# Products that nobody reads at the norms between the stages of a two-block transformer kernel

## The chip, the core and the metric

The kernel runs on one core of a Trainium2 chip. Five engines work side by side, each in its own program order, and wait for one another by semaphores: TensorE (PE, with its weight loads shown as PEld), VectorE (DVE), ScalarE (ACT), GpSimd (POOL) and SyncE (SP), which issues transfers. Matrix products land in PSUM, eight banks of 128 x 512 f32. TensorE's clock is granted at one of two levels, 2.4 and 1.2 GHz; the profile gives it as a share, 1.00 or 0.50. The metric is the time of one execution on the device in microseconds (us), lower is better.

## The reference

Two layers of a hybrid block (sliding-window attention beside an RWKV-7 mix, a gated FFN with a short convolution, and a gated embedding), then two layers of a second block (a pooling mixer beside latent attention, and a squared-ReLU FFN), then a last norm. There are 512 tokens of 1024 channels, all in f32. The norms and where they stand:

```python
def rmsnorm(x, g):
    y = xf * lax.rsqrt(jnp.mean(xf * xf, axis=-1, keepdims=True) + NORM_EPS)
    return y * g
# first block, per layer
h = rmsnorm(x, norm_mix_pre);  ... mixed from h ...
x = x + rmsnorm(mixed @ w_out, norm_mix_post)
h = rmsnorm(x, norm_ffn_pre);  ... u, ua, ub from h @ w_up ...
x = x + rmsnorm((gelu(ua) * ub) @ w_down, norm_ffn_post)
x = x + rmsnorm(sigmoid(x @ w_ple_gate) * (p_i @ w_ple), norm_ple)
# second block, per layer
h = rms_norm(x, ln1_g) * (1 + sc1) + sh1;  ...
x = x + g1 * (merged @ w_out)
h2 = rms_norm(x, ln2_g) * (1 + sc2) + sh2
x = x + g2 * (square(relu(h2 @ w_ff1)) @ w_ff2)
# at the end
rms_norm(x, final_g)
```

## The kernel before

Activations lie transposed: 8 tiles of 128 channels x 512 tokens (`xT`, `hh`, `hl`). Each f32 product is made of three: an operand is split into a high part (`hh`, `Whi`, rounded) and a low part (`hl`, `Wlo`, the rest), and TensorE adds high x high, low x high and high x low (L231). One weight tile of 128 x 1024, called a unit here, gives one output tile: 8 channel tiles by 3 products of 128 x 512, 24 in all. Units come from HBM in a fixed order (`raw`, issued by SP, L308); ACT makes `Whi` (L283) and GpSimd `Wlo` (L298), three slots deep. A first GEMM behind a norm takes two units at once (`split_pair`): per channel tile 6 products as soon as the `hl` of this tile is there, 48 in all; the 49th is the first of the third unit.

A norm goes through four engines:

- ACT squares a tile (L132, L161); TensorE sums it over channels by 16 one-column instructions per tile (`column_sums`, L177, into bank 7). Where a GEMM's outputs are summed (n2, n4, n5, and nx of the second block), DVE adds up six of the tiles first and TensorE has three groups of 16. At n3 and at nx of the first block there is one group per tile, eight in all, each behind the residual's tile (DVE L1812 and L1815).
- ACT takes the root (L145), DVE the reciprocal (L216, for nx L223).
- TensorE spreads the 4 columns of 1/root over a bank by four transposes (`norm_spread_pe`, L204, bank 6).
- DVE scales a tile (L391), ACT rounds it to `hh` (L364 or L366), DVE makes `hl` (L382 or L385): the split.

The names are n1 (before the mix), n2 (behind it in the first block, before the FFN in the second), n3 (before the FFN, first block), n4 (behind the FFN), n5 (behind the embedding's gate) and nx, the sums of the next layer's n1. Between nx and n1 a program block ends: all engines meet at a barrier, semaphores are cleared, and only then come n1's spread and the first weight loads of the new block. Behind n4 the products of `ph` and `pl` with the embedding's weights follow, which don't need the norm.

The order on each engine is the order in which the code is written; TensorE executes in that order, waits included.

Of the kernel before, what the change touches and what calls it, by code (L numbers as in the profile page):

```python
# [26 lines left out]
P = 128  # L27
# [3 lines left out]
KD = D // P  # L31
# [9 lines left out]
ADA_W, ADA_K = 512, 2  # L41
ADA_N = KD // ADA_K
MOD_BANK = 6


HEADS, KV, HD = 16, 4, 64
# [132 lines left out]
    return last  # L179


def norm_sum_pe(pe, s, b, name, i, n):

    pe.wait_ge(s[name + "_sq"], i + 1)
    column_sums(pe, b, b["sq"][:, i % 2], i == 0, i == n - 1).then_inc(s[name + "_ss"], 1)


def summed_squares_pe(pe, s, b, name):

    pe.wait_ge(s[name + "_ac"], KD - 3)  # L190
    column_sums(pe, b, b["sacc"], True, False)
    for i in (KD - 2, KD - 1):
        pe.wait_ge(s[name + "_sq"], i + 1)
        last = column_sums(pe, b, b["sq"][:, i % 2], False, i == KD - 1)
    last.then_inc(s[name + "_ss"], 1)


def norm_spread_pe(pe, s, b, name):

    if name != "n1":  # L200
        pe.wait_ge(s[name + "_rs"], 1)
    rt = b["rtn" if name == "n1" else "rt"]
    for c in range(BLK):
        last = pe.transpose(b["rstd"][:, c * P:(c + 1) * P], rt[:, c:c + 1].broadcast_to([P, P]), b["c"]("ident"))  # L204
    last.then_inc(s[name + "_sp"], 1)


def norm_pe(pe, s, b, name, n):
    for i in range(n):
        norm_sum_pe(pe, s, b, name, i, n)  # L210
    norm_spread_pe(pe, s, b, name)


def norm_dve(dve, s, name, b):
# [21 lines left out]
def tiles_of(high, low):  # L236

    return (lambda k: high[:, k]), (lambda k: low[:, k])
# [1817 lines left out]
def first_block(nc, b, stream, stream_after, ple, ada, positions):  # L2056
# [6 lines left out]
    with ExitStack() as ctx:  # L2063
        s, every = semaphores(ctx, nc, names)
# [42 lines left out]
        for layer in range(LAYERS):  # L2107
            enter_layer(b, layer, stream[layer], stream[layer + 1] if layer + 1 < LAYERS else stream_after[0])
            with nc.Block() as block:
# [50 lines left out]
                @block.tensor  # L2160
                def _(pe):
                    ring = Ring(s, b)
                    h = tiles_of(b["hh"], b["hl"])
                    norm_spread_pe(pe, s, b, "n1")
                    rwkv_pe(pe, s, b, ring)
                    pe.wait_ge(s["post_a"], POST_A(PAIRS - 1, "sd"))
                    attention_pe(pe, s, b, ring)
                    gated_pe(pe, s, b, ring, ((h, None), (h, None), (tiles_of(b["aoh"], b["aol"]), (s["ao_lo"], PAIRS)),
                                              (tiles_of(b["yrh"], b["yrl"]), (s["y_back"], 32 * PAIRS))))
                    pe.wait_ge(s["gate_a"], 16)  # L2170
                    project_pe(pe, s, b, ring, s["wo_p"], s["wo_z"], s["mx_lo"], "n2")
                    norm_spread_pe(pe, s, b, "n2")
                    norm_pe(pe, s, b, "n3", KD)
                    ffn_pe(pe, s, b, ring)
                    norm_spread_pe(pe, s, b, "n4")
                    for m in range(KD):
                        if m % 4 == 0:
                            w = ring.take(pe)
                        if m == 0:
                            pe.wait_ge(s["p_lo"], 1)  # L2180
                        if m >= 4:
                            pe.wait_ge(s["e_z"], m - 3)
                        split_matmuls(pe, b["ps"][:, m % 4], columns_of(w, 2, width=512, j=m % 4 * P), tiles_of(b["ph"], b["pl"]), 2) \
                            .then_inc(s["e_p"], 1)
                    pe.wait_ge(s["e_z"], 6)
                    project_pe(pe, s, b, ring, s["pg_p"], s["pg_z"], s["h3_lo"], "n5", (s["e_z"], KD))
                    norm_spread_pe(pe, s, b, "n5")
                    for i in range(KD):
                        norm_sum_pe(pe, s, b, "nx", i, KD)

                @block.scalar
                def _(act):
# [123 lines left out]
def second_pe(pe, s, b):  # L2316
    ring = Ring(s, b)
    norm_spread_pe(pe, s, b, "n1")
    pair = [ring.take(pe) for _ in range(2)]
    split_pair(pe, s["h1_lo"], [b["ps"][:, i] for i in range(2)], pair, b, s["z_p"])  # L2320

# [85 lines left out]
    gated2_pe(pe, s, b, ring)  # L2407
    pe.wait_ge(s["gate_a"], 16)
    project_pe(pe, s, b, ring, s["wo_p"], s["res1"], s["mx_lo"], "n2")
    norm_spread_pe(pe, s, b, "n2")  # L2410
    for key in FFN2[0]:
        if key[0] == "up":
            i = key[1]
            if i == 0:
                pair = [ring.take(pe) for _ in range(2)]
                split_pair(pe, s["h2_lo"], [b["ps"][:, x] for x in range(2)], pair, b, s["f1_p"])
            if i < 2:
                continue
            w = ring.take(pe)
            if i >= 4:  # L2420
                pe.wait_ge(s["f1_a"], i - 3)
            split_product(pe, b["ps"][:, i % 4], w, b).then_inc(s["f1_p"], 1)
        elif key[1] == PARTS2 - 1 and key[2] < OPEN:
            if key[2] == 0:
                last_down_pe(pe, s, b, ring, FT2)
        else:
            down_pe(pe, s, b, ring, key[1], key[2], FT2)
            if key[1] == PARTS2 - 1 and key[2] == KD - 1:
                summed_squares_pe(pe, s, b, "nx")


def gated2_pe(pe, s, b, ring):
# [690 lines left out]
```

## Time and profile before

| | us |
|---|---|
| median of 3 runs | 3971.61 |
| lowest and highest | 3971.05, 3975.33 |
| the profiled execution | 3976.66 |
| its span, first to last instruction | 3974.8 |
| TensorE busy (matmul) | 3763.6 |
| VectorE, ScalarE, GpSimd busy | 1909.9, 1601.3, 1716.6 |
| mean granted clock of TensorE | 0.973 |

A time line has a row for each run of like instructions: start, length, engine, source line, operation, output and inputs, sizes and count; in brackets the idle time before it and what ended that. A run of products is pipelined: the last one's tail is part of the row's length. A table of stretches gives the busy time of each engine in a stretch with the number of instructions, and the granted clock.

### The profile page before, as it was taken

What the parts mean: (1) busy time and instruction counts of PE and PEld (TensorE: products, weight loads), DVE (VectorE), ACT (ScalarE), POOL (GpSimd) and SP (SyncE); (2) the same over time, 40 slices, a digit from 0 to 9 for tenths busy, and PEclk for the clock granted to TensorE, in tenths of its full rate; (3) what the DMA queues carried; (4) which work ended last, traced back from release to release, by engine and by line L of the source; (5) the groups of instructions that cost most, each with busy time, mean ns of one, the idle gap of its engine ahead of it and who ended that gap; (6) DMA issues with size and microseconds to landing.
All of it is one profiled execution on the core that took longest, in us unless ns stands there. A gap on an engine that the chain in (4) does not pass through costs nothing. (4 is left out here: it accounts for less than half of the span.)

```text
span 3974.8 us, 71522 instructions
## 1 busy us (share of the span) xinstructions
PE 3763.6 (95%) x30328; PEld 3070.8 (77%) x30328; DVE 1909.9 (48%) x2978; ACT 1601.3 (40%) x2675; POOL 1716.6 (43%) x1088
## 2 busy tenths in 40 slices
PE   7999979999998999997999999899999999999998
PEld 6777758878887777776887888677878877787887
DVE  7777682255535767768215563535231123423112
ACT  5555353343334555526234233444332234433222
POOL 4555413434445555531443444453444435344443
PEclk9999989989999999998998999899999999999999
DMA  4111203235532211121433553221323322232332
GB/s 136 52 54 55 87 27 133 94 127 186 189 106 85 91 50 56 55 86 26 137 100 135 184 190 101 80 74 60 94 91 96 100 85 69 64 96 89 97 96 85
DMA packets 108749, 379.81 MB, mean 96 GB/s; under 512 B 12560, under 2 KB 12944, under 8 KB 107792
## 3 DMA queue, kind: packets, MB, share of 16 engines
q1 hardware_dynamic: 102816, 365.66, 28.5%
q10 hardware_dynamic: 5616, 9.58, 0.7%
q8 instruction: 241, 3.95, 0.4%
q14 instruction: 76, 0.62, 0.0%
HBM read 359.46 MB, written 15.73 MB: 94 GB/s over the span
## 5 line engine op out<-in xcount | busy, mean ns | idle before, releaser
L298 POOL TENSOR_TENSOR Wlo<-raw,Whi 128x1024 fp32r<-128x1024 f32 (+1 forms) x744 | 1383.0, 1871 | 1945.5 <-ACT Whi L283 1945.3
L231 PE MATMUL ps<-hh,Whi 128*128 128x512 f32 x2864 | 1152.2, 402 | 32.0 <-DVE hl L382 10.1
L231 PE MATMUL ps<-hl,Whi 128*128 128x512 f32 x2864 | 1126.1, 393 | 0.0
L231 PE MATMUL ps<-hh,Wlo 128*128 128x512 f32 x2864 | 1125.5, 393 | 0.1
L283 ACT ACTIVATE Whi<-raw 128x1024 fp32r<-128x1024 f32 x552 | 580.8, 1056 | 691.6 <-PE ps L231 618.0
L231 PEld LDWEIGHTS ps<-hh,Whi 128*128 128x128 f32 x2864 | 543.5, 190 | 161.5 <-issue 29.8
L231 PEld LDWEIGHTS ps<-hh,Wlo 128*128 128x128 f32 x2864 | 543.4, 190 | 115.9 <-issue 0.5
L231 PEld LDWEIGHTS ps<-hl,Whi 128*128 128x128 f32 x2864 | 544.2, 190 | 107.9 <-issue 1.9
L231 PE MATMUL ps<-gh,Whi 128*128 128x512 f32 x864 | 338.1, 391 | 4.1 <-POOL Wlo L298 4.1
L231 PE MATMUL ps<-gh,Wlo 128*128 128x512 f32 x864 | 336.6, 390 | 0.0
L231 PE MATMUL ps<-gl,Whi 128*128 128x512 f32 x864 | 336.6, 390 | 0.0
L1757 DVE TENSOR_TENSOR sg<-sg,ps 128x512 f32<-128x512 f32 x64 | 44.1, 688 | 369.5 <-PE ps L231 369.2
L1136 POOL TENSOR_TENSOR TM<-TD,const 128x256 f32<-128x256 f32 x192 | 162.8, 871 | 78.0 <-PE ps L718 43.8
L231 PEld LDWEIGHTS ps<-gh,Whi 128*128 128x128 f32 x864 | 162.3, 188 | 39.4 <-POOL Wlo L298 6.2
L231 PEld LDWEIGHTS ps<-gh,Wlo 128*128 128x128 f32 x864 | 162.3, 188 | 33.7
L231 PEld LDWEIGHTS ps<-gl,Whi 128*128 128x128 f32 x864 | 162.3, 188 | 33.2
L2688 DVE SCALAR_TENSOR_TENSOR xT<-ps,mod,xT 128x512 f32<-128x512 f32 x64 | 48.1, 752 | 281.1 <-PE ps L231 281.1
L1950 ACT ACTIVATE acc<-ps,par 128x512 f32<-128x512 f32 x88 | 68.6, 780 | 273.7 <-PE ps L231 273.7
L2678 DVE TENSOR_TENSOR gt<-gt 128x512 f32<-128x512 f32 x64 | 47.9, 749 | 256.9 <-ACT gt L2566 256.9
L2001 DVE SCALAR_TENSOR_TENSOR acc<-ps,par,acc 128x511 f32<-128x511 f32 x88 | 66.0, 750 | 198.0 <-ACT acc L1950 198.0
L1740 ACT ACTIVATE sg<-ps 128x512 f32<-128x512 f32 x64 | 38.3, 599 | 239.2 <-PE ps L231 239.2
L2566 ACT ACTIVATE gt<-ps 128x512 f32<-128x512 f32 x64 | 38.3, 598 | 213.0 <-PE ps L231 213.0
(360 smaller groups left out, 5746.3 us busy)
## 6 DMA issues: line engine op xcount, KB each, us to landing
raw<-in_stream SPq DMA_DIRECT2D x554, 512.0 KB, 3.6
ada<-in_ada SPq DMA_DIRECT2D x96, 512.0 KB, 4.5
park_x<-xT SPq DMA_DIRECT2D x2, 2048.0 KB, 7.2
park_yh<-yh ACTq DMA_DIRECT2D x16, 256.0 KB, 2.1
park_yl<-yl ACTq DMA_DIRECT2D x16, 256.0 KB, 2.4
xT<-park_x SPq DMA_DIRECT2D x2, 2048.0 KB, 8.2
yrh<-park_yh SPq DMA_DIRECT2D x16, 256.0 KB, 5.1
yrl<-park_yl SPq DMA_DIRECT2D x16, 256.0 KB, 5.2
```

The source lines that it names most:

```text
L231: last = pe.matmul(ps, left[a](k), right[c](k), start=start and k == 0 and i == 0, stop=stop and k == n - 1 and i == 2)
L283: act.activation(self.b["Whi"][:, weight_slot(self.b, u)], self.b["raw"][:, raw_slot(self.b, u)], ACT.Copy).then_inc(self.s["w_hi"], 1)
L298: last = pool.tensor_tensor(b["Wlo"][:, slot, part], b["raw"][:, raw_slot(b, u), part], b["Whi"][:, slot, part].bitcast(F32), SUB)
L1136: pool.tensor_tensor(blocks(b["TM"][:, h, l % 2]), blocks(b["TD"][:, h]), lvl[:, l].broadcast_to([P, BLK, CB]), MUL) .then_inc(s["inv_g"], 1)
L1740: act.activation(b["sg"][:, i], b["ps"][:, i], ACT.Sigmoid).then_inc(s["gate_a"], 1)
L1757: dve.tensor_tensor(b["sg"][:, i], b["sg"][:, i], b["ps"][:, 4 + i], MUL).then_inc(s["gate_v"], 1)
L1950: act.activation(b["acc"][:, slot], b["ps"][:, slot], ACT.Identity, scale=b["p"]("cw2", j * FT + i), bias=b["p"]("cb", j * FT + i)).then_i ...
L2001: dve.scalar_tensor_tensor(out=b["acc"][:, slot, 1:TOK], in0=b["ps"][:, slot, 0:TOK - 1], scalar=b["p"]("cw1", j * FT + i), in1=b["acc"][: ...
L2566: act.activation(b["gt"][:, i % 4], b["ps"][:, i % 4], ACT.Relu).then_inc(s["f1_a"], 1)
L2678: dve.tensor_tensor(b["gt"][:, i % 4], b["gt"][:, i % 4], b["gt"][:, i % 4], MUL).then_inc(s["f1_v"], 1)
L2688: dve.scalar_tensor_tensor(out=b["xT"][:, m], in0=b["ps"][:, 4 + i % 3], scalar=b["mod"][:, 40 + m:41 + m], in1=b["xT"][:, m], op0=MUL, op ...
```

## The change

A helper `idle_products` issues n products of two constants (the identity and a tile of ones, 128 x 128 each, f32) into PSUM bank 5, columns 0 to 127. Nothing reads them, and they wait for nothing. They stand at three kinds of place: 6 between the last column sum of a norm and what waits for its root (`IDLE_ROOT`), 4 before each column sum of n3 and of the first block's nx, 10 before the first of them (`IDLE_SUM`, and two thirds of `IDLE_SPLIT`), and 16 between a spread and the first GEMM product behind it (`IDLE_SPLIT`). That is 154 per layer of the first block and 44 per layer of the second, 396 in all. No other instruction changes, on any engine.

```diff
+IDLE_BANK = 5
+IDLE_ROOT, IDLE_SUM, IDLE_SPLIT = 6, 4, 16
+def idle_products(pe, b, n):
+    for _ in range(n):
+        pe.matmul(b["ps"][:, IDLE_BANK, 0:P], b["c"]("ident"), b["c"]("ones"), start=True, stop=True)
-def norm_pe(pe, s, b, name, n):
+def idle_sums_pe(pe, s, b, name, n):
     for i in range(n):
+        idle_products(pe, b, 2 * IDLE_SPLIT // 3 if i == 0 else IDLE_SUM)
         norm_sum_pe(pe, s, b, name, i, n)
-    norm_spread_pe(pe, s, b, name)
+    idle_products(pe, b, IDLE_ROOT)
...
                     norm_spread_pe(pe, s, b, "n1")
+                    idle_products(pe, b, IDLE_SPLIT)
                     rwkv_pe(pe, s, b, ring)
...
                     project_pe(pe, s, b, ring, s["wo_p"], s["wo_z"], s["mx_lo"], "n2")
+                    idle_products(pe, b, IDLE_ROOT)
                     norm_spread_pe(pe, s, b, "n2")
-                    norm_pe(pe, s, b, "n3", KD)
+                    idle_sums_pe(pe, s, b, "n3", KD)
+                    norm_spread_pe(pe, s, b, "n3")
+                    idle_products(pe, b, IDLE_SPLIT)
                     ffn_pe(pe, s, b, ring)
+                    idle_products(pe, b, IDLE_ROOT)
                     norm_spread_pe(pe, s, b, "n4")
+                    idle_products(pe, b, IDLE_SPLIT)
...
                     project_pe(pe, s, b, ring, s["pg_p"], s["pg_z"], s["h3_lo"], "n5", (s["e_z"], KD))
+                    idle_products(pe, b, IDLE_ROOT)
                     norm_spread_pe(pe, s, b, "n5")
-                    for i in range(KD):
-                        norm_sum_pe(pe, s, b, "nx", i, KD)
+                    idle_sums_pe(pe, s, b, "nx", KD)
...
# second block
     norm_spread_pe(pe, s, b, "n1")
+    idle_products(pe, b, IDLE_SPLIT)
...
     project_pe(pe, s, b, ring, s["wo_p"], s["res1"], s["mx_lo"], "n2")
+    idle_products(pe, b, IDLE_ROOT)
     norm_spread_pe(pe, s, b, "n2")
+    idle_products(pe, b, IDLE_SPLIT)
...
                 summed_squares_pe(pe, s, b, "nx")
+                idle_products(pe, b, IDLE_ROOT)
```

TensorE before, in the first block from the end of the mix's projection over n2 and n3 to the first GEMM of the FFN (`sacc` and `sq` are the squares, `rt` the reciprocal root, `hh`, `hl`, `Whi`, `Wlo` the parts):

```order
L177 MATMUL ps<-const,sacc 64x1 x8
L177 MATMUL ps<-const,sq 64x1 x16
L204 MATMUL ps<-const,rt 128x128 x4
L177 MATMUL ps<-const,sq 64x1 x64
L204 MATMUL ps<-const,rt 128x128 x4
L231 MATMUL ps<-hh,Whi 128x512
```

The same place now; L187 are the new products, and L177, L204 and L231 are L179, L212 and L240:

```order
L179 MATMUL ps<-const,sacc 64x1 x8
L179 MATMUL ps<-const,sq 64x1 x16
L187 MATMUL ps<-const 128x128 x6
L212 MATMUL ps<-const,rt 128x128 x4
L187 MATMUL ps<-const 128x128 x10
L179 MATMUL ps<-const,sq 64x1 x8
L187 MATMUL ps<-const 128x128 x4
...
L187 MATMUL ps<-const 128x128 x6
L212 MATMUL ps<-const,rt 128x128 x4
L187 MATMUL ps<-const 128x128 x16
L240 MATMUL ps<-hh,Whi 128x512
```

Nothing changed its order; every spread, every column sum from n3's first on and the first GEMM product stand behind a set of new products. At a block's end, here between nx of the second layer and n1 of the second block (the two branches are the end of one program block and the start of the next, with the barrier between them), the six stand before the barrier:

```order
L179 MATMUL ps<-const,sq 64x1 x8
L187 MATMUL ps<-const 128x128 x6
L2118 UNCONDITIONAL_BRANCH
L2823 UNCONDITIONAL_BRANCH
L212 MATMUL ps<-const,rtn 128x128 x4
L187 MATMUL ps<-const 128x128 x16
L240 MATMUL ps<-hh,Whi 128x512
```

Before, the column sums were TensorE's last work ahead of that barrier.

## Rows read from the trace of the kernel before

**Rows 1.** The page: the span, and TensorE's clock in 40 slices.
```profile
span 3974.8 us, 71522 instructions
...
PEclk9999989989999999998998999899999999999999
```

**Rows 2.** Time line, TensorE: spreads of n2, n4 and n5, five of eight.
```profile
821.68 1.12 PE L204 MATMUL ps<-const,rt 128*128 128x128 f32 x4 [0.58 <-DVE rt L216]
...
1281.62 0.65 PE L204 MATMUL ps<-const,rt 128*128 128x128 f32 x4 [0.57 <-DVE rt L216]
...
2103.35 0.65 PE L204 MATMUL ps<-const,rt 128*128 128x128 f32 x4 [0.58 <-DVE rt L216]
...
2498.06 1.12 PE L204 MATMUL ps<-const,rt 128*128 128x128 f32 x4 [0.58 <-DVE rt L216]
...
2910.90 1.12 PE L204 MATMUL ps<-const,rt 128*128 128x128 f32 x4 [0.65 <-DVE rt L216]
```

**Rows 3.** Stretches of time: busy time of each engine, and the clock.
```profile
core 0: us, PE busy (x) PEld busy (x) DVE busy (x) ACT busy (x) POOL busy (x), PEclk, DMA share, GB/s
2907.20:2910.50 3.30, 2.58 (x53) 1.97 (x51) 0.82 (x2) 0.83 (x2) 0.00 (x0) 1.00 0.55 159
2910.60:2920.70 10.10, 7.26 (x19) 5.54 (x20) 8.45 (x13) 4.27 (x6) 0.00 (x0) 0.50 0.01 2
821.60:845.40 23.80, 15.97 (x149) 13.38 (x150) 18.75 (x30) 9.08 (x15) 0.00 (x0) 0.50 0.06 21
```

**Rows 4.** Time line at n2 of the second block, layer 1.
```profile
2909.62 0.63 PE L177 MATMUL ps<-const,sq 128*64 128x1 f32 x16 [0.48 <-ACT sq L161]
...
2914.56 0.77 PE L231 MATMUL ps<-hh,Whi 128*128 128x512 f32 x1 [2.54 <-DVE hl L382]
...
2924.21 2.40 POOL L298 TENSOR_TENSOR Wlo<-raw,Whi 128x1024 fp32r<-128x1024 f32 x1 [17.89 <-ACT Whi L283]
...
2928.45 0.39 PE L231 MATMUL ps<-hh,Whi 128*128 128x512 f32 x1
```

**Rows 5.** Time line, TensorE, at n3 of the first block, layer 1.
```profile
825.03 1.02 PE L177 MATMUL ps<-const,sq 128*64 128x1 f32 x16 [2.23 <-ACT sq L132]
...
831.94 1.02 PE L177 MATMUL ps<-const,sq 128*64 128x1 f32 x16 [0.36 <-ACT sq L132]
...
839.81 0.77 PE L231 MATMUL ps<-hh,Whi 128*128 128x512 f32 x1 [2.39 <-DVE hl L385]
...
853.46 0.39 PE L231 MATMUL ps<-hh,Whi 128*128 128x512 f32 x1
```

**Rows 6.** Attention: f32 products on the time line, and stretches as in rows 3.
```profile
2685.27 4.03 PE L2403 MATMUL ps<-PT,vtok 128*64 128x128 f32 x20
...
2685.30:2688.60 3.30, 3.30 (x17) 3.30 (x17) 3.23 (x9) 1.97 (x7) 3.06 (x4) 0.50 0.00 0
2688.70:2692.00 3.30, 3.29 (x17) 2.03 (x15) 3.30 (x7) 1.09 (x5) 3.05 (x4) 1.00 0.00 0
558.80:562.00 3.20, 3.20 (x20) 2.87 (x22) 3.17 (x4) 1.60 (x3) 0.00 (x0) 0.50 0.00 0
562.20:565.50 3.30, 2.65 (x34) 1.98 (x30) 3.20 (x7) 3.02 (x13) 0.00 (x0) 1.00 0.00 0
```

**Rows 7.** Time line between nx of layer 1 and n1 of layer 2.
```profile
1295.54 0.18 DVE L223 RECIPROCAL rtn<-rtn 128x4 f32<-128x4 f32 x1 [2.08 <-ACT rtn L145]
...
1297.13 1.09 PE L204 MATMUL ps<-const,rtn 128*128 128x128 f32 x4 [1.93 <-PEq L117]
...
1305.32 0.69 DVE L385 TENSOR_TENSOR hl<-t,hh 128x512 fp32r<-128x512 f32 x1
...
1307.32 2.40 DVE L385 TENSOR_TENSOR hl<-t,hh 128x512 fp32r<-128x512 f32 x1 [0.53 <-ACT hh L366]
```

**Rows 8.** Time line behind n4's spread, layer 1.
```profile
1217.30 2.35 POOL L2151 TENSOR_TENSOR pl<-pT,ph 128x1024 fp32r<-128x1024 f32 x1 [4.29 <-ACT ph L2222]
1217.55 2.65 DVE L1815 TENSOR_TENSOR xT<-xT,t 128x512 f32<-128x512 f32 x1
```

## Prediction, before the changed kernel was run

> **What bounds the kernel now.** I read the page first [rows 1]: the span is 3974.8 us, and TensorE's granted clock is below full speed in some slices only. The profiled execution took 3976.66 us, 5.05 us above the median of the three timed runs (3971.61); every difference below is worked out inside the profiled execution and then laid on that median. Second, the time line of the eight spreads of n2, n4 and n5, of which five stand in [rows 2]: four transposes took 0.65 us where the clock was 2.4 GHz, and 1.11 or 1.12 us where it was 1.2 (at half clock also those at 2562.94 and 3604.20, at full that at 1216.08). Third, busy time and clock by stretch [rows 3]: from 821.6 to 845.4 and from 2910.6 to 2920.7 the clock stood at 0.50, although VectorE, not TensorE, sets the pace of most of it. What that costs is the part where TensorE has the 48 products of the first two weight tiles to do. In the first block they began at 839.81 and the 49th began at 853.46 [rows 5], 13.65 us, of which 5.6 us (839.81 to 845.4) at 1.2 GHz. If a product takes p at full and 2p at half clock, 5.6/2p + 8.05/p = 48, so p = 0.226 us, and 48 at full clock would be 10.85 us. Behind that pair TensorE is back to back, so what is gained or lost at the 49th product is carried on.
>
> **What one of the new products costs.** Nobody waits for them, but TensorE works in order, so whatever stands behind them waits. None of that shape (128x128 by 128x128, f32) is in the trace. Nearest is the run of 20 f32 instructions with 128 columns at 2685.27 [rows 6], 4.03 us, of which 3.38 us at half clock: 16 at 0.214 is 3.4, four at 0.109 is 0.4, plus a tail of 0.2. An f32 product in the source is two such instructions, so a product is 0.22 us at full clock and 0.43 at half. The transposes bound it from the other side: 0.65 against 1.12 us for four [rows 2] gives 0.118 each. A set of 6 is thus 1.3 (2.6) us, of 16 3.5 (6.9), of 10 2.2 (4.3), of 4 0.87 (1.7). Column sums of one tile: 0.63 us at full and 1.02 at half [rows 4, 5], 0.48 and 0.9 without the tail.
>
> **Can they hold the clock?** In the stretch before 2910.5 TensorE counted as busy 2.58 of 3.30 us at clock 1.00 [rows 3], and yet it fell: what ran last were 48 one-column sums, and the longest idle piece shown there is 0.48 us [rows 4]. The Trainium skill says in "TensorE: Matmul & The Clock Gate", section "Why this matters for your kernels", that throughput is kept by leaving no long idle gap between bursts; by that rule the norms would be cured by any instruction stream and the sum would be the "held" one below, 3966. The trace does not agree that gaps decide. I take from the rows that column sums do too little, and that products of this kind do enough, since the clock rose from 0.50 to 1.00 while the 20 instructions of [rows 6] ran. But the six products come only behind the last sum. In five of the eight spreads the transposes already ran at half clock [rows 2]: there the fall came within 0.6 us of the last sum (2910.90 less 0.65 is the sum's end, the fall was at 2910.5), before the six can have done much. In the other three it came behind the spread, and there they can prevent it. So each place has two ends, held and fallen.
>
> **Second block, n2 (twice).** Held: the six start at 2910.1 and end at 2911.4; the spread waits for them instead of the reciprocal, and takes 0.65 instead of 1.12, so it ends at 2912.05 against 2912.02. The sixteen fill 2911.8 to 2915.3; the first GEMM product starts 0.7 us later than 2914.56 [rows 4]. 48 at 0.226 end at 2926.1, but the low part of the third tile is there only at 2924.21 + 2.40 = 2926.6 [rows 4]: 2926.7 against 2928.45, a gain of 1.75; layer 2 alike, 1.6. Fallen: two of the six at full clock, four at 0.43, a spread of 1.12: it ends at 2913.35, 1.35 late; VectorE's chain and the third tile move with it, 2928.0 against 2928.45, a gain of 0.45, and in layer 2 a loss of 0.2.
>
> **First block, n2 and n3 (twice).** The residual hands a tile to the sums every 1.38 us (1.02 busy and 0.36 idle [rows 5]); sums and four products at full clock are 0.48 + 0.87 = 1.35, so they just fit. The ten before the first sum fit its wait of 2.2 us (825.03). The last sums are 0.4 us shorter, the six delay the spread by 0.6 and it is 0.45 shorter: end 0.2 earlier. The sixteen let the first product start at 840.5, 48 end at 851.4 against 853.46: gain 2.0. In layer 2 the clock had risen sooner by itself: gain 1.0. Fallen at n2: the spread is 1.3 to 1.8 us late, the sixteen run at full clock again: gain 0.5 and 0.
>
> **Block ends (three into an n1, one into the last norm).** The barrier waits for the last engine. That was VectorE's reciprocal at 1295.54, and the spread came at 1297.13 [rows 7]. Now TensorE's six end later than that, by 0.6 to 1.0 us. Behind the barrier the weight loads start too, and one split step waits for them and then beside GpSimd (2.40 us at 1307.32, where the one before took 0.69 [rows 7]), so a faster TensorE gains little there. Held: losses 0.2, 0, 0.1 and 0.4, in all 0.7. Fallen: the six take 2.6, and at n5 the spread and the residuals behind it are late too: 2.7, 2.2, 1.9 and 1.9, in all 8.7.
>
> **Before the e products (n4, twice).** The spread comes 0.55 us later at full clock. It costs nothing: VectorE's second step there was stuck beside GpSimd's subtraction anyway (2.65 us at 1217.55, against 2.35 us from 1217.30 [rows 8]). Fallen, the spread is 1.8 us late and the first product 2.9: 1.3 each, 2.6. **Start:** sixteen products at half clock delay the first GEMM by 2 to 4 us, but they also bring the rise forward: loss 0.2, between 0 and 1.0.
>
> **Sum.** All held: -6.4 + 0.7 + 0 + 0.2 = -5.5, or 3966.1. All fallen: -(0.5 + 0 + 0.45 - 0.2) + 8.7 + 2.6 + 1.0 = +11.5, or 3983.1. Falling where it fell before: first block -1.3 (between its ends, since 821.68 ran at half clock but the fall came late) and -1.0, second block -0.45 and +0.2, block ends +0.2, +2.2, +0.3, +0.4, n4 0 and +1.3, start +0.2: +2.05. The place of the fall is not tied to the program: the same norm of the two layers ran its spread at 1.12 (821.68) and at 0.65 us (2103.35) [rows 2]. So I lean a little to the middle of the ends (+3.0): +2.4, 3974.0 us. On the profiled execution's own time that is 3979.1.
>
> **Rivals.** (1) *Held everywhere*, 3966.1. For it: three of the eight spreads at full clock. Against: in five the fall comes with the last sum. (2) *Fallen everywhere*, 3983.1. (3) *Slower: the clock stays down through the sums of n3 or nx.* Sums and four products at half clock are 0.9 + 1.7 = 2.6 us against the 1.38 that VectorE gives; seven times 1.25 is 8.7 us, and with the late spread 12 us at each of four norms: 3986 for one, 4022 for all. It decides at one point: whether the clock is up again before the first sum. Against it: six products, spread and ten products are 7.7 us without a gap at half clock, more than the 5.6 us that GEMM products needed. The Trainium skill says in the same page, Part 4, that transposes do not count as activity for the clock; by that rule the spread breaks this run and the rival is likelier. The trace speaks against it: from 558.8 to 562.0 only transposes and short f32 products ran, at clock 0.50, and from 562.2 on it was 1.00 [rows 6]. (4) *The products don't count for the clock at all:* then all sums run so, some 4050; the 20 instructions of [rows 6] speak against it.
>
> **Chances.** Mixed falls, as forecast: 0.55 (3970 to 3979). Held: 0.17. Fallen everywhere or nearly: 0.18. Low clock through sums: 0.08. Not counted: 0.02. A measurement here can tell about 0.2%, 7.9 us. Held comes to -5.5, inside it; I give faster 0.12 for errors in my terms. Slower is the upper half of fallen, rivals 3 and 4 and a little of the mixed case: 0.26. Same: 0.62. The range reaches from held to fallen: 3966 to 3984.
>
> **What the changed kernel's profile would show.** Product groups of 16 lasting 3.5 us (6.9 if at half clock); spreads of 0.65 us; sums and four products every 1.38 us with TensorE idle under 0.1; clock 1.00 from n3's first sum to the split and 10.9 us for 48 products, with a wait for the third tile's low part in the second block. At block ends TensorE, not VectorE, is last at the barrier, and the spread follows the reciprocal by 2.2 us or more instead of 1.6. Wrong I would be if the clock fell inside the sums, or if it held at all of the five early places, or if a product took much more than 0.22 us.

## The result, and the profile after

The changed kernel takes 3994.02 us (median; 3988.5 to 3997.57) beside 3973.47 for the kernel before: 1.0054 times as long, 95% interval 1.0042 to 1.0066. It is 21 us slower, outside the predicted range (3966 to 3984). The profiled execution took 3992.09 us, its span is 3989.6.

The page of the changed kernel, span and granted clock in 40 slices, answers to [rows 1]:
```profile
span 3989.6 us, 73106 instructions
...
PEclk9999989999999999998999999999999999999999
```
Of five slices that stood at 8 three are at 9; the mean clock rose from 0.973 to 0.987. So the change did what it says, and the kernel got slower all the same. The clock was not the thing to look at; the time between two marks in the program was.

TensorE at n2 and n3 of the first block, layer 1 (start us, us, then as in [rows 2]; L187 are the new products, two instructions each, L179 the column sums, L212 a spread, L240 GEMM products):
```profile
825.14 2.29 PE L187 MATMUL ps<-const 128*128 128x128 f32 x12
827.22 1.06 PE L212 MATMUL ps<-const,rt 128*128 128x128 f32 x4
828.08 2.98 PE L187 MATMUL ps<-const 128*128 128x128 f32 x20
...
832.64 0.63 PE L179 MATMUL ps<-const,sq 128*64 128x1 f32 x16
833.20 1.16 PE L187 MATMUL ps<-const 128*128 128x128 f32 x8
834.29 0.63 PE L179 MATMUL ps<-const,sq 128*64 128x1 f32 x16
...
842.54 0.63 PE L179 MATMUL ps<-const,sq 128*64 128x1 f32 x16
843.11 1.60 PE L187 MATMUL ps<-const 128*128 128x128 f32 x12
...
844.55 0.60 PE L212 MATMUL ps<-const,rt 128*128 128x128 f32 x4
...
848.48 0.47 PE L240 MATMUL ps<-hh,Whi 128*128 128x512 f32 x1
...
859.48 0.39 PE L240 MATMUL ps<-hh,Whi 128*128 128x512 f32 x1
```
Read the starts, 832.64 and 834.29: a tile of sums and its four products take 1.65 us, where VectorE hands over a tile every 1.38 [rows 5]. The last line is the 49th product: 11.00 us after the first, 13.65 before [rows 5]. So 2.65 us are won there, and by then 4.56 have been lost. Layer 1, each step counted from the one before it and set against the same step of before, by the starts: n2's spread +1.43 from its first sum (the six, half of them at 1.2 GHz); the first sum of n3 0.42 further (the ten); seven intervals of 1.65 instead of 1.38, +1.87; n3's spread +0.42 (the six); the first GEMM product +0.43 (the sixteen); the 49th -2.65. In all +1.92.

The stretches, as in [rows 3]:
```profile
826.00:842.50 16.50, 16.50 (x199) 15.47 (x198) 10.88 (x16) 5.04 (x8) 0.00 (x0) 0.90 0.08 26
842.50:859.40 16.90, 16.90 (x113) 14.97 (x113) 11.06 (x17) 6.67 (x11) 2.39 (x1) 1.00 0.00 1
```
TensorE had no idle time left in the sums, at a clock of 0.90. In [rows 3] it was busy for 15.97 of 23.8 us, at 0.50. From the engine that waited it has become the bound.

The first block end (n5, nx, n1 of layer 2), layer 1:
```profile
1287.37 1.02 PE L179 MATMUL ps<-const,sq 128*64 128x1 f32 x16 [1.69 <-ACT sq L163]
1288.31 2.93 PE L187 MATMUL ps<-const 128*128 128x128 f32 x12
1291.03 1.06 PE L212 MATMUL ps<-const,rt 128*128 128x128 f32 x4
...
1307.10 1.61 PE L187 MATMUL ps<-const 128*128 128x128 f32 x12
...
1310.09 0.62 PE L212 MATMUL ps<-const,rtn 128*128 128x128 f32 x4 [1.38 <-PEq L119]
...
1320.73 0.39 PE L240 MATMUL ps<-hh,Wlo 128*128 128x512 f32 x1
1323.82 0.50 PE L240 MATMUL ps<-hh,Whi 128*128 128x512 f32 x1 [2.71 <-DVE hl L394]
```
The clock had fallen at n5's last sum: the six took 2.93 us and the spread, itself at half clock, comes 2.46 later than 1281.62 [rows 2]. nx's spread is 3.56 later still. Behind it TensorE, at full clock, has done 30 of the pair's 48 products by 1321, those of five channel tiles, and waits 2.7 us for the sixth tile's low part. VectorE could start on that only behind ACT's rounding (2.13 us idle), which in turn stood behind the split of a weight tile that had waited for its transfer, and then took 2.35 us for it beside GpSimd, as in [rows 7]:
```profile
1319.74 1.06 ACT L292 ACTIVATE Whi<-raw 128x1024 fp32r<-128x1024 f32 x1 [2.55 <-DMA raw<-in_stream]
...
1321.42 2.35 DVE L394 TENSOR_TENSOR hl<-t,hh 128x512 fp32r<-128x512 f32 x1 [2.13 <-ACT hh L375]
```
Right behind this wait the clock fell once more; the stretches with the clock:
```profile
1320.80:1324.20 3.40, 0.69 (x4) 0.34 (x3) 2.74 (x2) 1.04 (x3) 2.34 (x1) 1.00 0.00 0
1324.30:1327.50 3.20, 3.20 (x9) 2.43 (x8) 1.54 (x3) 0.63 (x1) 0.10 (x1) 0.50 0.42 159
```
The 49th product is 1.88 us later relative to the first, not 2.65 earlier. This block end costs 8.5 us: 2.46 and 3.56 for the two spreads, 0.56 for the sixteen behind the second, and 1.88.

### The profile page after: what moved, and what is told of

It reads as the page before. It is cut to its first block and busy times, and to the rows that moved or that the text cites. A ratio compares the mean times of both kernels' runs of the same rounds, so it can differ in the third digit from the quotient of the medians.

```text
span 3989.6 us, 73106 instructions
## 1 busy us (share of the span) xinstructions
PE 3828.5 (96%) x31120; PEld 3141.4 (79%) x31120; DVE 1902.8 (48%) x2978; ACT 1601.8 (40%) x2675; POOL 1715.7 (43%) x1088
## 5 line engine op out<-in xcount | busy, mean ns | idle before, releaser
L240 PE MATMUL ps<-hh,Whi 128*128 128x512 f32 x2864 | 1144.3, 400 | 16.9 <-ACT wS L893 9.3
L240 PE MATMUL ps<-hl,Whi 128*128 128x512 f32 x2864 | 1118.8, 391 | 0.0
L240 PE MATMUL ps<-hh,Wlo 128*128 128x512 f32 x2864 | 1118.7, 391 | 0.0
L240 PEld LDWEIGHTS ps<-hh,Whi 128*128 128x128 f32 x2864 | 538.9, 188 | 143.0 <-issue 18.9
L240 PEld LDWEIGHTS ps<-hh,Wlo 128*128 128x128 f32 x2864 | 539.0, 188 | 114.3 <-issue 0.2
L240 PEld LDWEIGHTS ps<-hl,Whi 128*128 128x128 f32 x2864 | 539.5, 188 | 106.8 <-issue 1.9
L240 PE MATMUL ps<-gh,Whi 128*128 128x512 f32 x864 | 337.9, 391 | 3.8 <-POOL Wlo L307 3.8
L240 PE MATMUL ps<-gh,Wlo 128*128 128x512 f32 x864 | 336.5, 390 | 0.0
L240 PE MATMUL ps<-gl,Whi 128*128 128x512 f32 x864 | 336.5, 389 | 0.0
L240 PEld LDWEIGHTS ps<-gh,Whi 128*128 128x128 f32 x864 | 162.2, 188 | 38.9 <-POOL Wlo L307 5.5
L240 PEld LDWEIGHTS ps<-gh,Wlo 128*128 128x128 f32 x864 | 162.2, 188 | 33.7
L240 PEld LDWEIGHTS ps<-gl,Whi 128*128 128x128 f32 x864 | 162.2, 188 | 33.4
L727 PEld LDWEIGHTS ps<-X,TM 64*64 64x64 f32 x2560 | 82.0, 135 | 54.1 <-issue 29.6
```

Source lines behind the costliest of these rows:

```text
L240: last = pe.matmul(ps, left[a](k), right[c](k), start=start and k == 0 and i == 0, stop=stop and k == n - 1 and i == 2)
L727: return pe.matmul(b["ps"][half(u), bank, block(c)], left[:, block(c)], right[:, block(c)], start=True, stop=True)
```

## The experiments

Every kernel here is told by five numbers: how many products stand behind the very first spread (start), between the last sum and a spread (six), ahead of the first sum of n3 and nx (ten), ahead of each other sum (four), and between a spread and the first GEMM product (sixteen). The first and the last are one constant (`IDLE_SPLIT`) in all kernels but g1, g2 and g3. The edit is small, for instance of the run with three in place of four:
```
-IDLE_ROOT, IDLE_SUM, IDLE_SPLIT = 6, 4, 16
+IDLE_ROOT, IDLE_FIRST, IDLE_SUM, IDLE_SPLIT = 6, 10, 3, 16
...
-        idle_products(pe, b, 2 * IDLE_SPLIT // 3 if i == 0 else IDLE_SUM)
+        idle_products(pe, b, IDLE_FIRST if i == 0 else IDLE_SUM)
```
In g1, g2 and g3 a constant of its own stands behind n1's spread in the first block, and that line is run for both layers: g1 and g3 have the sixteen at the start and behind n1 of layer 2 (g1's trace has 64 instructions of these products, the last at 1302.6 us), g2 lacks them at both. Where their expectations say "the very first spread", read both.

"Norms" below is worked out from a kernel's trace: the times of the marks (first sum or first spread of a norm to the 49th product behind it, with the start and the end of the program) against those of the first trace of before, summed over all norms. "Rest" is the same for all else, where the change puts nothing. The ratio is to before on the same chip.

| kernel | start, six, ten, four, sixteen | median us | ratio (95%) | norms | rest |
|---|---|---|---|---|---|
| before, second trace | 0 0 0 0 0 | 3967.3 (one) | | +0.5 | -9.8 |
| changed | 16 6 10 4 16 | 3994.0 | 1.0054 (1.0042 to 1.0066) | +17.9 | -3.1 |
| e6, changed again | the same | 4000.4 (one) | | +23.0 | +0.8 |
| g4, a third time | the same | 3997.9 | 1.0065 (1.0051 to 1.0078) | +21.6 | +1.5 |
| e1 | 16 6 10 0 16 | 3994.7 | 1.0056 (1.0038 to 1.0074) | +19.5 | -1.2 |
| e2 | 16 6 10 2 16 | 4008.3 | 1.0082 (1.0067 to 1.0098) | +25.4 | +6.9 |
| e7 | 16 6 10 3 16 | 3980.2 | 1.0023 (1.0013 to 1.0033) | +9.1 | -7.2 |
| f2 | 16 6 10 8 16 | 4020.8 (one) | | +47.1 | -3.0 |
| f3 | 0 0 0 4 0 | 4011.7 (one) | | +43.3 | -8.3 |
| f1 | 0 6 0 0 0 | 3987.1 | 1.0035 (1.0023 to 1.0047) | +15.8 | -4.7 |
| e3 | 16 0 10 4 16 | 3986.0 | 1.0033 (1.0023 to 1.0044) | +9.9 | -1.2 |
| e4 | 16 0 0 0 16 | 3979.1 | 1.0013 (1.0003 to 1.0022) | -0.4 | -7.5 |
| e8 | 8 0 0 0 8 | 3965.4 | 0.9987 (0.9977 to 0.9996) | -7.9 | -8.7 |
| f4 | 8 0 10 3 8 | 3970.1 | 0.9991 (0.9982 to 1.0000) | -3.7 | -3.0 |
| g1 | 16 (and at n1 of layer 2) 0 0 0 0 | 3976.4 | 1.0007 (0.9998 to 1.0016) | +0.2 | -5.9 |
| g2 | 0 (nor at n1 of layer 2) 6 10 4 16 | 3992.5 | 1.0048 (1.0032 to 1.0063) | +12.2 | +6.5 |
| g3, g1 again | the same as g1 | 3973.4 (one) | | +1.0 | -4.2 |

**What repeats and what does not.** Two traces more of the two kernels, unchanged.

> The kernel before, unchanged, for a second trace. The question is what the stretches that the change does not touch do between two executions of one program. In the traces so far the start of the first column sum at the end of the attention (819.05 us in before) moved by +0.5 to +7.0 us between kernels, measured from the 49th product of the first stage, and that of the second layer (2100.72) by -0.8 to -6.8. Theory A (where the clock falls in those stretches is chance): the two marks move by up to 6 us here too, and the norms by less than 0.5 us each. Theory B (the change moves them): both marks stay within 1 us of before's first trace.

> The changed kernel, unchanged, for a second trace. Theory A (losses at the norms are the pace of TensorE and repeat, the rest is chance): the spread of n3 and nx comes again 2.7 to 3.6 us late against before, the gain at the following 48 products is again 2.1 to 2.6 us wherever the third tile is there, all norms together +15 to +19 us, and the attention stretches differ from the first trace by up to 6 us. The loss of 1.88 us behind the first block end's n1 (1300 to 1314 us) is a second fall of the clock while TensorE waited; it may or may not repeat. Theory B (the places of the falls make the loss): the norms' sum differs by more than 5 us between the two traces.

In before's second trace the norms sum to within 0.5 us of the first, though two of them moved more than theory A allowed (-0.9 and +1.1 in the second block); elsewhere it differs by 9.8, 5.8 of it in the second attention alone, while the first ended 0.6 late. Of the 5.8, 3.6 lie at one place: in the first trace TensorE stood still for 1.83 us there, for nothing that the profile shows, and the clock fell right behind it; in the second trace neither happened. The row and the stretch in before, then the same stretch in its second trace:
```profile
1417.81 0.33 PE L718 MATMUL ps<-XT,Wc 64*64 64x64 f32 x4 [1.83 <-issue]
...
1418.90:1422.30 3.40, 3.40 (x9) 2.63 (x8) 3.36 (x6) 0.95 (x3) 1.61 (x3) 0.50 0.22 41
```
```profile
1418.90:1422.30 3.40, 3.40 (x123) 2.75 (x125) 3.37 (x6) 3.12 (x7) 3.40 (x4) 1.00 0.00 0
```
The changed kernel's n2 and n3 of layer 1 cost +1.9 in all three traces, of layer 2 +2.9, the first block end +8.5, +8.4, +8.8. Between the three, norms differ by up to 5.1 us, at block end 2 and the last norm above all, where the six ran at full or at half clock. That is just past the 5 us of theory B, and +23.0 and +21.6 lie above the 19 and 20 us that theory A gave. So the larger part of the norms' loss, about 18 us, is of the kernel and repeats (theory A), up to 5 us hang on where the clock falls, and a single trace's rest is of the execution. The column "norms" also follows the measured medians: sums of 3, 4 and 8, +9.1, +20.8 (the mean of three) and +47.1, against +9, +21 to +26 and +49 us beside before. It does not replace them: e2's and g2's medians lie 8 us above their norms, and the traced executions of e4 and e8 were the fastest of ten, 10 and 5 us below the median.

**Between the sums.** Four runs vary this number, one has it alone.

> The changed kernel without the four products between the column sums of n3 and nx (seven times four at each of four norms); the ten before the first sum, the six and the sixteen stay. In the changed kernel's trace each sum with its four products takes 1.65 us, where the residual gives a tile every 1.385: 7 to 8 times 0.27, 2.1 us per norm, 8.5 in all. Theory A (the sums' pace is the largest mis-sized term): 8 us below the changed kernel, about 3986; or a little less gain if the clock falls during the sums, since a sum at half clock (1.02) still fits 1.385. Theory B (what costs is the six products that stand before spreads and barriers): no change, 3994.

> The changed kernel with two products instead of four between the sums. At full clock a sum is 0.48, two products 0.44 and the switch between them 0.28: 1.2, which fits 1.385; at half clock 0.9 + 0.85 + 0.3 = 2.0, which does not. Theory A: 8 us below the changed kernel, 3986, with the spread behind the sums at full clock (0.65). Theory B: 3994. If the clock falls in the sums it is above 3994.

> As the changed kernel, with three products in place of four between the column sums of n3 and nx. In the changed kernel a tile of sums took 1.65 us (0.63 to 0.65 the sums, 0.89 four products, the rest in going from one to the other), where VectorE hands one over every 1.38 us. Theory A (the pace of TensorE there is the loss): with three, 1.65 - 0.22 = 1.43 us a tile, 0.05 above VectorE's, so seven intervals cost 0.3 in place of 1.9 us at each of the four norms; the spread of n3 comes 1.0 us late in place of 2.7, and if the clock holds the kernel takes 6 to 7 us less than the changed one, 3987. Theory B (three leave the clock to fall, as two did, and then sums and products run at half clock, 2.6 us or more a tile with three): as slow as with two, 4000 to 4008, spread of n3 3 to 4 us late.

> The changed kernel with eight products in place of four between column sums. The suspected cost doubled: four took 1.65 us a tile, three 1.43, so a product is 0.22 and the sums with the turn from one kind to the other are 0.76. Theory A: eight give 0.76 + 1.78 = 2.54 us a tile, at each of the four norms seven intervals of 2.54 - 1.65 = 0.89, 6.2 us more than the changed kernel, 25 us in all, so 4012 to 4028 (executions of one kernel differ by up to 8 us); the clock holds through the sums. Theory B (not the pace of TensorE but the places of the clock's falls make the loss): no more than 10 us above the changed kernel.

> The kernel before with four products ahead of each column sum of n3 and nx but the first, and none elsewhere. Theory A (the pace is the loss, whatever surrounds it): if the clock is up or comes up during the first tiles, 1.65 us a tile, the spreads of n3 and nx 1.9 to 2.6 us late; if it is down at the first sum it takes 2.6 us a tile or more until it rises, up to 4 us late. The first GEMM product behind them then starts at full clock and gives 2.6 us back per place where VectorE lets it: between -1 and +2 us at each of the four places, 0 to +6 in all. Theory B (the clock does not rise at all on four products and sums): 2.6 us a tile throughout, 8 us and more at each of the four, over 30 us in all.

TensorE in n3 of layer 1, with three products (e7), with eight (f2):
```profile
829.58 0.63 PE L179 MATMUL ps<-const,sq 128*64 128x1 f32 x16
830.14 0.94 PE L187 MATMUL ps<-const 128*128 128x128 f32 x6
831.00 0.63 PE L179 MATMUL ps<-const,sq 128*64 128x1 f32 x16
```
```profile
835.40 0.63 PE L179 MATMUL ps<-const,sq 128*64 128x1 f32 x16
835.96 2.05 PE L187 MATMUL ps<-const 128*128 128x128 f32 x16
837.94 0.63 PE L179 MATMUL ps<-const,sq 128*64 128x1 f32 x16
```
A tile takes 1.43, 1.65 and 2.54 us with three, four and eight: 0.22 for a product, and 0.76 for the sixteen sum instructions and the turns. The sums themselves are 0.56 of it (829.58 to 830.14), so turning back from products to sums costs 0.2. Eight cost 23 us more than the changed kernel (3997.4, the mean of its three values in the table), as theory A said (25); three take 12 us less by the ratios, more than the 6 to 7 expected: the pace is 6 of it. In e7's trace the second fall behind the first block end is missing as well (the 49th product there -0.75 instead of +1.88).

Less is not simply better. With none (e1) the sums run at VectorE's pace, but alone they don't keep the clock, and it falls before the last; with two (e2) the same happens, and then the last sums, the six, the spread and the first of the sixteen run at half clock. So e1's 3994.7 is the number of theory B, but not for its reason, and e2 came 14 us above the changed kernel, as its last sentence had it. TensorE in e1 and in e2, n3 of layer 1:
```profile
838.75 0.74 PE L179 MATMUL ps<-const,sq 128*64 128x1 f32 x16 [0.75 <-ACT sq L134]
840.13 1.02 PE L179 MATMUL ps<-const,sq 128*64 128x1 f32 x16 [0.64 <-ACT sq L134]
...
843.85 2.93 PE L187 MATMUL ps<-const 128*128 128x128 f32 x12
```
```profile
839.11 0.63 PE L179 MATMUL ps<-const,sq 128*64 128x1 f32 x16
839.68 0.95 PE L187 MATMUL ps<-const 128*128 128x128 f32 x4
840.55 1.02 PE L179 MATMUL ps<-const,sq 128*64 128x1 f32 x16
841.50 1.22 PE L187 MATMUL ps<-const 128*128 128x128 f32 x4
```
In e2 TensorE had no idle time before this fall (busy for all of 834.3 to 839.7, at clock 1.00), so no gap made it. e1 shows that the loss is not bought back by taking the sums' products away alone: what they held, the six and sixteen lose. The sums alone (f3) are the worst of all, by theory B. TensorE, then the stretch:
```profile
831.67 1.02 PE L179 MATMUL ps<-const,sq 128*64 128x1 f32 x16
832.62 2.07 PE L187 MATMUL ps<-const 128*128 128x128 f32 x8
834.62 1.02 PE L179 MATMUL ps<-const,sq 128*64 128x1 f32 x16
```
```profile
826.00:846.00 20.00, 20.00 (x167) 18.55 (x166) 8.53 (x13) 4.41 (x7) 0.00 (x0) 0.50 0.00 1
```
TensorE was at work for 20 us without a gap, and the granted clock stayed at 1.2 GHz. A tile took 2.95 us, seven intervals 11 us more: 10.5 to 11.2 us from spread to spread at each of the four norms. The advice quoted ahead of the result, from the Trainium skill, "TensorE: Matmul & The Clock Gate", section "Why this matters for your kernels", to leave no long idle gap, was kept to in this row, and the clock did not come back; with this mix being busy is not enough.

**Before the spread, and behind it.**

> The changed kernel without the six products before spreads and barriers; the ten, four and sixteen stay. Theory B: the six delay ten spreads by 0.8 (full clock) to 2.3 us (half) and four barriers by 0.8: 8 to 15 us less than the changed kernel, 3979 to 3986. Theory A: at most 4 us less, because what a late spread costs is partly given back by the 48 products at full clock, and without the six the sixteen run at half clock more often.

> The kernel before with six products between the last column sum and the spread at every norm, and none elsewhere. Prices the six alone. In the kernels with sixteen behind the spread too, the spread came 1.4 to 1.9 us late at n2 and n4 of the first block and 2.5 at n5 where the six ran at 1.2 GHz, 0.7 to 1.0 in the second block; without them (two kernels with none before the spread) 0.0. Theory A (they delay the spread and buy nothing that the work behind would not buy): eight spreads late by 0.7 to 2.5 us each, 12 us, and a little of it hidden where VectorE or a transfer is late anyway; 6 to 14 us above before. Theory B (the six, by themselves, keep or bring back the clock, and the first GEMM products start at full clock): the 48 products take 11.0 instead of 13.7 us, 2 us back at each of nine places, so -4 to +2 us.

> Only the sixteen products behind a spread. Sums and roots are as in the kernel before. The sixteen take 3.5 us at full and 6.9 at half clock against a wait of 2.4 to 2.6 us, so each of nine places starts its first product 1 to 4.4 us late and runs the 48 at full clock (3 us less where they ran at half clock throughout). Theory A: 3974 to 3980. Theory B: the same, 3974 to 3980. A time near 3994 would say that the sixteen are the cause.

Without the six the spreads that follow a GEMM's sums are at most 0.24 us late (e3), with them alone 0.7 to 2.7 (f1). The six alone cost 14 us by the ratio (theory A). They come out ahead by 0.8 to 1.6 us at n4 of layer 1 and at the second block's n2, and lose 1.9 and 4.5 at n2 and n3, 5.0, 3.5 and 3.0 at the three block ends; at the first of these they run at half clock (12 instructions in 2.93 us), and the sums behind them still do (1.02 us). Taken out of the changed kernel (e3) they give 8 us back (theory B, at the edge of its range). The sixteen alone (e4) come out at about nothing in the trace, and 5 us slower by the medians. TensorE behind n3's spread in e4:
```profile
836.62 1.11 PE L212 MATMUL ps<-const,rt 128*128 128x128 f32 x4 [0.58 <-DVE rt L225]
837.53 4.74 PE L187 MATMUL ps<-const 128*128 128x128 f32 x32
842.02 0.48 PE L240 MATMUL ps<-hh,Whi 128*128 128x512 f32 x1
```
The sixteen overhang the wait of 2.39 us [rows 5]: the first GEMM product comes 5.40 us behind the spread, before 3.50, so 1.9 later, and the pair then takes 2.64 less. The gain lies in the products that fill the wait; those beyond it are paid for one by one. Hence eight:

> The kernel before with eight products between a spread and the first GEMM product, and none elsewhere (no products before a spread or between sums). With sixteen, the first GEMM product came 1.9 to 2.9 us late (the sixteen ran at half clock for 6 us and more), the 49th 2.6 us earlier relative to it: about 0.7 us net at each of nine places. Theory A (only the overhang of the sixteen past the wait costs): eight are 3.4 to 3.5 us at half clock, as long as the wait of 2.4 to 3.5 us, so the first product comes 0 to 0.8 us late; the clock rises at the same place or up to 1 us later; a net gain of 0.7 to 1.7 us at a place, 6 to 12 us in all in the traces, a median of 3966 to 3974. Theory B (the rise needs the long run of sixteen): the clock rises where it rose before, the gain is gone and the time is before's, 3974 to 3977.

> Ten products ahead of the first column sum of n3 and nx, three ahead of each other one, eight behind each spread, none before a spread: the fillers in the sizes that the waits had in the traces. Theory A (each filler that fits its wait is free, and a norm that is entered at full clock gives 2.6 us back instead of the 1.8 that eight alone gave): the spreads of n3 and nx 0.3 to 0.9 us late, the first GEMM product not later than before, 48 products in 11.0 us; 0 to 1.5 us better than eight alone at each of four places, 3960 to 3966 beside a before of 3971 to 3974. Theory B (with no products between n2 or n5 and the ten, the clock is down when the sums start, and the ten at half clock, 4.3 us, overrun their wait of 2.2): spreads of n3 and nx 2 to 3 us late, as in the kernel without products before the spreads, and 1 to 4 us above eight alone.

TensorE behind n3's spread in e8:
```profile
837.63 1.11 PE L212 MATMUL ps<-const,rt 128*128 128x128 f32 x4 [0.58 <-DVE rt L225]
838.54 3.62 PE L187 MATMUL ps<-const 128*128 128x128 f32 x16
841.81 0.77 PE L240 MATMUL ps<-hh,Whi 128*128 128x512 f32 x1
842.38 0.63 PE L240 MATMUL ps<-hl,Whi 128*128 128x512 f32 x1
842.81 0.63 PE L240 MATMUL ps<-hh,Wlo 128*128 128x512 f32 x1
843.24 0.55 PE L240 MATMUL ps<-hh,Whi 128*128 128x512 f32 x1
```
Eight fill the wait and a little more (the first product 0.68 late) and the clock is up at its fourth, 1.4 us behind the first; the pair takes 1.82 less. Net 1.15 us at n3. Over all norms it is 7.9 us, by the medians 0.13% (0.04 to 0.23), some 5 us: a small gain, just clear of the noise, as theory A had it; it is faster than both kernels. Adding ten and three (f4) brings no more, against its theory A: the spreads of n3 and nx come 1.0 to 1.5 us late for it, the pair behind n3 takes 11.7 us and not 11.0, and it can't be told from e8 (the medians are of two chips).

**The stretch that the change does not touch.** With the changed kernel the first attention ended 4.0 us late in two traces.

> The kernel before with the sixteen products behind the very first spread and no others. Theory A (they move the clock's falls in the stretches behind): the start of the column sum at 819.05 comes 2 to 7 us late, and the kernel takes 3 to 5 us more than before, 0.1%. Theory B (chance of the execution): the sum comes 0 to 1 us late, the time is before's within 1 us.

> The sixteen at the start alone, a second trace. Theory A: the sum at 819.05 again 2 to 7 us late. Theory B: 0 to 1 us late, or once late and once not.

> The changed kernel without the sixteen products behind the very first spread. Theory A: the sum at 819.05 comes within 1 us of before, the rest is the changed kernel's, so it takes 3 to 5 us less than the changed kernel. Theory B: the sum comes 0 to 7 us late by chance, the time is the changed kernel's within 1 us.

> The changed kernel a third time, beside the others on the same chip. Its norms are again 17 to 20 us later than before in the sum, whatever the clock does elsewhere; the sum at 819.05 is 4 us late by theory A, 0 to 7 by theory B; the time 3991 to 4000.

Measured from the 49th product of the first stage to the sum at 819.05: +0.6 and +0.1 with the sixteen at the start alone (g1, g3), +4.4 in the changed kernel without them (g2), +0.7 in the changed kernel's third trace (g4). e3 and e4, whose programs are the same up to n2, had +6.0 and +0.5; e1, e2, e7 and f2, the changed kernel up to that place, +6.9, +7.0, +0.9 and +6.2. The first column sum on TensorE at that place, in e3 and then in e4:
```profile
825.13 0.63 PE L179 MATMUL ps<-const,sacc 128*64 128x1 f32 x16
```
```profile
819.63 0.63 PE L179 MATMUL ps<-const,sacc 128*64 128x1 f32 x16
```
So the shift does not hang on the products at the start: chance of the execution (theory B). g1's time, 4 us above before, is what theory A gave, but its interval holds theory B's as well, and its second execution (g3) took 3973.4. By the time, g2 is 5.4 us below g4, which theory A had asked for; its trace has the difference at the first block end, +3.1 instead of +8.8. There the edit itself acts: without the sixteen behind n1 of layer 2 the first GEMM product comes 1.0 us sooner behind the spread, and the 49th is +0.3 instead of +2.0. The other 3.0 us come before, with n5's spread (0.80 late instead of 2.46) and the first sum behind it, where the program is the same; whether that is chance again, one trace doesn't tell.

## Why the prediction was wrong

The norms, forecast by the mixed case and measured in the three traces of the changed kernel, in us:

| place | forecast | measured |
|---|---|---|
| start | +0.2 | +0.1, +0.3, +0.65 |
| first block, n2 and n3, layers 1 and 2 | -1.3, -1.0 | +1.9 (thrice), +2.9 (thrice) |
| n4, layers 1 and 2 | 0, +1.3 | +0.9 to +1.0, +1.5 |
| block end 1 | +0.2 | +8.5, +8.4, +8.8 |
| block end 2 | +2.2 | +2.3, +5.1, +2.4 |
| block end 3, last norm | +0.3, +0.4 | +0.6; +0.5, +2.9, +1.9 |
| second block, n2, layers 1 and 2 | -0.45, +0.2 | +0.1, -0.1, 0.0; -1.4, -1.4, -0.1 |
| sum | +2.05 | +17.9, +23.0, +21.6 |

**The step that failed first** is "they just fit": sums and four products were put at 0.48 + 0.87 = 1.35 us, and took 1.65. The product was right (0.22), and so are 0.48 us for sums behind sums, as before's trace has them at n2:
```profile
819.05 0.63 PE L177 MATMUL ps<-const,sacc 128*64 128x1 f32 x16
819.54 0.61 PE L177 MATMUL ps<-const,sq 128*64 128x1 f32 x16
```
What was put at nothing is the turn between the two kinds of instruction: sums with products behind them take 0.56 start to start, 0.08 more, and turning back from products to sums takes 0.2. With 0.03 us of room, an error of 0.3 turned a filler into the bound: 1.87 us at each of four norms, 7.5 in all. The runs with three, four and eight show this term by itself.

**The six.** At the five places where before ran its spread at half clock the fall was taken to come too early for them, and at the other three (1216.08, 1281.62, 2103.35) "they can prevent it". It went the other way: in all three traces of the changed kernel the six and the spread ran at half clock, wholly or in part, at just these three, and the spreads came 1.4 to 1.8, 2.5, and 1.5 us late, while at n5 of layer 2 and at n2 of the second block's layer 2, where before's had fallen, it held in two traces of the three (0.7 to 0.8 late). n2's spread in the first block was 1.43 and 1.55 late in the two layers, as the fallen case had it (1.3 to 1.8), not the mixed one. Why the clock falls at one place sooner than at another no run shows.

**The ten and the sixteen at n3.** The ten were to fit the wait before the first sum; they start behind a late spread, partly at half clock, and put the sum 0.42 us further in layer 1 and 0.78 in layer 2. What stands behind the sums came nearly as forecast: n3's spread starts 0.41 later but is shorter and ends 0.1 earlier (0.2 forecast), and with the sixteen the first GEMM product comes 0.84 late (0.7 forecast).

**The block end.** Layer 1's end was put at +0.2. What was mis-sized: the fall at n5, taken as late there because the spread in [rows 2] ran at 0.65 us, came with the last sum (2.46 us, and half clock for the spread and part of the ten, which puts the first sum 1.1 us further); then the sums' pace, 1.9; the six at the barrier, 0.6, as forecast; the sixteen behind nx's spread, 0.6; and the wait for the sixth channel tile's low part, which was named ("a faster TensorE gains little there"), but not that the clock would fall right behind that wait, so that the 49th product is another 1.9 later. The last repeated in all three traces of the changed kernel.

**What was right.** The product at 0.22 us (six at half clock took 2.72 us, start to start, 2.6 forecast); 48 GEMM products in 11.0 us at full clock (10.85 to 10.9 forecast), a gain of up to 2.65 at a place; the clock's rise while six products, the spread's transposes and ten products ran, at n2 of layer 1. The second block's n2, where the third weight tile's low part is the bound, came within 0.6 of its forecast in layer 1; in layer 2 it came out up to 1.6 better, the clock having held. Held everywhere (rival 1) did not come, nor did rival 2: some places fell and some held, as in the mixed case, but not the ones it named, and the whole scale was wrong. Rival 3 did not occur in the changed kernel, yet its mechanism is real: f3 is this rival, 2.95 us a tile and 11 us a norm, forecast 2.6 and 8.7 to 12. Its deciding point, the clock before the first sum, was right too, and the ten are what brings it up there: in e3, with ten and no six, a tile of sums and four products took 1.65 us again. Rival 4 is out. None of the three signs by which the prediction would be wrong came (a fall inside the sums, a clock that held at all five early places, a product well above 0.22); what did not come was its row "every 1.38 us with TensorE idle under 0.1".

Of the 16 to 21 us between the forecast sum and the measured ones the pace is 7.5 in every trace; the rest is what the late spreads cost in front of the sums and at the block ends. The slow side of the range was built from where the clock falls alone, so it ended at 3983, and the pace of TensorE at full clock, an arithmetic of 0.03 us, had no rival of its own.

## What to carry to other kernels

A filler is free only as long as it ends before the wait that it fills does, counted with its cost at the low clock and with the turn between two kinds of instruction; in a loop that another engine paces at 1.38 us, 1.35 is not a fit but a risk. Size fillers by the shortest wait of each place (eight here, 3.3 us at half clock, where the first GEMM product stood 3.5 us behind the spread's start), put none where somebody waits for TensorE right behind them, and judge by the time between marks of the program, not by the mean clock: it was highest in kernels that were slower. Take two traces of the same kernel before reading a shift of a few us in a stretch that an edit doesn't touch.

## What the runs showed of the hardware

- TensorE worked for 20 us without a gap on column sums and f32 products, at a granted clock of 0.50 throughout (f3); with six, spread and ten products ahead, the same mix ran at 2.4 GHz to its end (the changed kernel). In these runs the mix kept a clock that was up, and did not raise one that was down.
- Between column sums, two products were too few to keep the clock (e2, which lost it with TensorE busy throughout), three were enough at all four norms of e7 and of f4 (a tile every 1.43 us).
- Turning from one-column sums to f32 products cost 0.08 us at full clock and turning back 0.2; a product cost 0.22, the same from three to eight in a row. At half clock four products and the turn took 2.00 us (f3, 832.62 to 834.62).
- In one program, the same stretch of 786 us differed by 5.8 us between two executions; 3.6 of it were one wait of TensorE that the profile puts down to nothing and a fall of the clock right behind it.
